# A table set with both Exp and Ln, loaded once per stretch, and 26 more ticks in the Exp form of the gelu

## What is computed

```python
h = rmsnorm(x, norm_mix)
q_sb, k_sb, v_sb, q_sw, k_sw, v_sw, q_mem, gates = split_projection(h, w_in, b_gate)
# stick-breaking attention
log_keep = where(mask, -softplus(z), 0); weight = where(mask, exp(log_sigmoid(z) + log_between), 0)
# windowed attention (softmax with sinks) and attention over memory tokens (softmax)
x = x + merge(o_sb, o_sw, o_mem, gates, w_o_sb, w_o_sw, w_o_mem, w_out)
x = x + peer_ffn(rmsnorm(x, norm_ffn), w_peer_q, peer_keys, peer_u, peer_v)
# peer_block, per row: 8 heads, the 16 best of 128 x 128 experts each
g = softmax(best)
a = gelu(einsum('thkd,td->thk', u_tab[idx], xb))
out = einsum('thk,thkd->td', g * a, v_tab[idx])
```

## Time and profile before

| | us |
|---|---|
| median of 3 runs | 4570.85 |
| lowest, highest | 4563.27, 4574.06 |
| the profiled execution | 4568.99 |
| its span, first to last instruction | 4567.2 |

### The profile page before, as it was taken

How to read it: one execution, slowest core, us unless ns; L and a number is a source line. 1 busy time by engine, 2 the same in 40 slices (tenths; PEclk the granted TensorE clock), 3 DMA queues, 4 the chain that set the end, 5 groups by cost and what they waited for, 6 DMA issues and landing times.

```text
span 4567.2 us, 47872 instructions
## 1 busy us (share of the span) xinstructions
PE 3318.5 (73%) x16665; PEld 1485.3 (33%) x16665; DVE 2543.6 (56%) x6300; ACT 1999.6 (44%) x4853; POOL 1249.0 (27%) x1167
## 2 busy tenths in 40 slices
PE   8988987766666999886775565699988555555555
PEld 4565653222222445432322222244443111111111
DVE  1321148546655674684565645676458577576544
ACT  4531024656887322325567788832232222222222
POOL 0000013212112333332221212233333444444443
PEclk9869998787777999987887777799999776777777
DMA  5222359766655999998865556699999999999999
GB/s 201 68 68 92 128 204 412 286 255 249 217 206 213 401 416 409 413 382 317 307 255 188 215 213 224 248 416 414 415 404 378 412 416 416 416 412 417 417 421 382
DMA packets 230819, 1407.40 MB, mean 308 GB/s; under 512 B 26144, under 2 KB 34080, under 8 KB 77088
## 3 DMA queue, kind: packets, MB, share of 16 engines
q0 software_dynamic: 165888, 1208.03, 66.4%
q1 hardware_dynamic: 64688, 196.30, 11.6%
HBM read 1384.58 MB, written 20.58 MB: 308 GB/s over the span
## 4 chain that ended last, share of the span: by engine, by line
PE 39%; DMA 20%; ACT 18%; DVE 18%; issue 5%; POOL 1%; SPq 0%; DVEq 0%; ACTq 0%; POOLq 0%
DMA ring<-in_experts_dram,idx 20%; PE ps L1177 11%; DVE ring L1740 7%; PE ps L1106 7%; PE ps L911 4%; PE ps L1149 4%; PE ps L1111 4%; PE ps L1126 3%; ACT L1396 3%; ACT L1394 3%; ACT diag L1414 2%; ACT L1316 1%; ACT wgt L1408 1%; PE ps L1084 1%; PE ps L906 1%
## 5 line engine op out<-in xcount | busy, mean ns | idle before, releaser
L1177 PE MATMUL ps<-ring,diag 64*64 64x512 f32 x9216 | 1429.6, 748 | 1001.1 <-ACT diag L1414 984.2
L862 POOL DMA_INDIRECT ring<-in_experts_dram,idx x1152 | 1243.6, 1079 | 3141.5 <-PE ps L1177 2511.7
L1740 DVE CUSTOM_DVE_ANT_0 ring<-ring,xp 128x1024 f32<-128x1024 f32 x1152 | 1389.4, 1224 | 828.0 <-DMA ring<-in_experts_dram,idx 807.8
L1177 PEld LDWEIGHTS ps<-ring,diag 64*64 64x64 f32 x9216 | 351.8, 158 | 1906.4 <-ACT diag L1414 1344.9
L1400 ACT ACTIVATE act_<-hid 128x2 f32<-128x2 f32 x416 | 84.6, 203 | 1632.3 <-DVE hid L1740 1614.5
L1106 PE MATMUL ps<-hx,over 128*128 128x384 f32 x1152 | 400.1, 496 | 7.3 <-DMA over<-in_w_gate_o_dram 7.3
L1414 ACT ACTIVATE diag<-const,wgt 128x64 f32<-128x64 f32 x1152 | 337.9, 340 | 18.8
L911 PE MATMUL ps<-over,hx 128*128 128x512 f32 (+1 forms) x720 | 314.5, 590 | 0.0
L1106 PEld LDWEIGHTS ps<-hx,over 128*128 128x128 f32 x1152 | 214.4, 191 | 202.4 <-issue 70.8
L1149 PE MATMUL ps<-hx,over 128*128 128x384 f32 x768 | 264.6, 494 | 1.2 <-ACT hx L1352 1.2
L1531 DVE SCALAR_TENSOR_TENSOR over<-ps,over 128x512 f32<-128x512 f32 x76 | 52.6, 692 | 300.7 <-ACT over L1316 292.1
(11 more groups left out here) (217 smaller groups left out, 3336.9 us busy)
## 6 DMA issues: line engine op xcount, KB each, us to landing
over<-in_w_gate_o_dram SPq DMA_DIRECT2D x72, 768.0 KB
over<-in_w_in_dram SPq DMA_DIRECT2D x15, 2048.0 KB
over<-in_w_q_dram SPq DMA_DIRECT2D x24, 1024.0 KB
ring<-in_experts_dram,idx POOLq DMA_INDIRECT x1152
over<-in_w_out_dram SPq DMA_DIRECT2D x12, 1024.0 KB
oq<-in_x_prompt_dram SPq DMA_DIRECT2D x16, 512.0 KB, 15.6
x_scratch<-oq SPq DMA_DIRECT2D x9, 512.0 KB
over<-in_w_mem_kv_dram SPq DMA_DIRECT2D x2, 2048.0 KB
```

Source lines behind the costliest of these rows:

```text
L862: i = nc.gpsimd.indirect_dma_start(out=ring[:, j % RING, :], out_offset=None, in_=A["experts"], in_offset=bass.IndirectOffsetOnAxis(ap=idx ...
L1177: last = nc.tensor.matmul(acc[ROWS[r ^ h], h, :], diag[ROWS[r], j % 4, :], ring[ROWS[r], j % RING, DM + h * HB:DM + (h + 1) * HB], start=( ...
L1740: last = nc.vector.tensor_tensor_reduce(out=rows, in0=rows, in1=xp[:, :], scale=1.0, scalar=0.0, op0=ALU.mult, op1=ALU.add, accum_out=hid[ ...
```

## The change

A set of ACT's tables that has both Exp and Ln, `natural_log_exp_and_others`, is asked for by name at the begin of the program, at each tick where a stretch of the Exp form begins, and in `front` before the second norm's Ln. And `exp_form()` takes the first RANK_LEAD + 2 = 28 ticks too (26 of them had the Gelu form), so the stretches become 0 to 93 and 192 to 283.

```diff
+LOGS = "natural_log_exp_and_others"
...
     for T in range(NT * NB):
         to = done + PACES[1 + T]
-        out.append(any(done <= b and to > a for a, b in spans[1:]))
+        out.append(T < RANK_LEAD + 2 or any(done <= b and to > a for a, b in spans[1:]))
         done = to
...
                     if tau == f.mean_at:
+                        nc.scalar.preload_act_table_set(LOGS)
                         act.wait_ge(meaned, g + 1)
...
             advance = walk(project, attend, front)
+            nc.scalar.preload_act_table_set(LOGS)
             advance(0)
...
                     c = recent(tick)
+                    if EXP_FORM[T] and not (T and EXP_FORM[T - 1]):
+                        nc.scalar.preload_act_table_set(LOGS)
                     act.wait_ge(dots, T + 1)
```

## The result

The changed kernel takes 4212.75 us (median) against 4570.51 us, 0.9218 of it, 95% interval 0.92 to 0.9236. Its profiled execution took 4211.32 us (span 4209.2). The forecast was 4240 with a range of 4150 to 4340: right in direction, 27 us too high. One of the changed kernel's four executions took 6292.23 us, at a granted clock of 1.00, for a reason that nothing here shows; the ratio leaves it out, and without it the median is 4211.32.

What follows compares the result with a forecast made beforehand. Packed transfers bound the first ticks and fronts; in projections and attention ACT's table loads made ticks late. Terms -59 - 56 - 67 - 137 - 9 - 5 + 8 = -325 from 4569 gave 4244, said as 4240, range 4150 to 4340.

Steps and rivals of the forecast that it cites:

- The loads are ACT's time, 1.31 us a switch, and go: Whole kernel: each table switch costs ACT 1.31 us; some 30 of 600 loads stay once one set holds both functions.
- Their worth is what lies on the chain: Each stage gains only its loads on the chain, not all 769.7 us, limited by the busiest other engine's floor.
- Attention 2: Attention of group 2 under the ticks, 589.8 us: chain loads 158.1, DVE floor 438, so -152, taken as -137.
- Attention 1: Attention of group 1 under the ticks, 377.4 us: chain loads 74.3, DVE floor 298, so -74, taken as -67.
- a tenth off: Both attention stretches: gain cut by a tenth because DVE and PE would wait for each other; a choice, not a row.
- The projections' floor: Projections of groups 1 and 2: PE's busy time over 0.92 leaves 233 and 232 us, so -59 and -56.
- Before tick 0: Stretch ahead of the first tick: chain loads of 6.5 and 2.6 us go, -9 us.
- Fronts: Fronts 1 and 2, at `mean_at`: two loads leave, -5 us for both, or 0 where packed DMA takes it back.
- The first 26 ticks: Ticks 0 to 25 switched to the Exp form: +8 us, bounds -3 to +29; 0.4 of DVE's 17.4 us counted.
- Whole chain and faster clock: Rival: all chain loads go and PE's clock rises in denser attention, about 4150 us; 15%.
- Another path close under the chain: Rival: in attention the DVE-PE exchange may hold the ticks, half the loads' time stays, 4390 us; 14%.
- The preload does not hold: Rival: loads still precede every Ln and Exp, first 26 ticks go from 6.1 to 9.4 us, +86, 4655 us; 3%.

Runs made afterwards that it cites:

- e5: Changed kernel with first 26 ticks back in the Gelu form, but DVE still doing its four Exp-form instructions there, results unused: 4204.82 us, 0.9205; that stretch 167.0 us.
- e2: Kernel before the change, with the Exp form in the first 28 ticks and no preload: 4590.31 us, 1.0057 of the kernel before.
- e3: Changed kernel with one load of the already loaded table before the gelu's first Exp in each of 186 Exp-form ticks: 4313.72 us, 0.9456 of the kernel before.

## Why the prediction was right, and where it was off

- **The loads are ACT's time, 1.31 us a switch, and go.** Right: 31 left of 600 (some 30 forecast), and ACT's busy time fell by 717.8 us (1999.6 to 1281.8; 569 loads x 1.283 = 730, less the added ACTIVATEs).
- **Their worth is what lies on the chain.** Right, and it is the step that carried the forecast. But the sums took the loads of the printed part of each row: 60.2, 74.3, 61.4 and 158.1 us where the whole chains hold 69.4, 77.2, 68.1 and 167.0. In three of the four stretches the drop was the whole of that within 5% (72.6, 76.2, 65.6), in attention 2 0.81 of it (136.0).
- **Attention.** Attention 2: 137 forecast, 136.0 measured. Attention 1: 67 forecast with a tenth off, 74 without it, 76.2 measured. The tenth was a choice and not a row; it was wrong in the one and hit in the other, where 152 would have stood without it. That the term of attention 2 came out to 1 us is luck in part.
- **The projections' floor was the most mis-sized term.** The terms added to -325, measured was -358.0: 33 us, 23 of them here (13.6 and 9.6), 9 in attention 1, 10 before tick 0, and 9 back in the fronts and last ticks. I took PE's busy time of before as fixed (214.34 us) and allowed a share of 0.92, which gave 233. PE reached only 0.88 of 219.8, but its busy time fell to 194.42 for the same 887 matmuls. With that time the same floor is 211 us in both projections and binds nothing; the stage less the loads of its whole chain is then 292.4 - 69.4 = 223.0 and 288.1 - 68.1 = 220.0, against 219.8 and 222.5 measured. It took both errors: with the whole row read and the old floor the forecast would still have been 233 and 232. The matmuls' groups in projection 1, before and after:

```profile
L911 PE MATMUL ps<-over,hx 128*128 128x512 f32 (+1 forms) x240 | 109.2, 607 | 0.0
...
L912 PE MATMUL ps<-over,hx 128*128 128x512 f32 (+1 forms) x240 | 99.0, 559 | 0.0
```

  559 ns in place of 607 for each, at a granted clock of 0.95 in place of 0.85. The runs form a row in projection 1: clock 0.85, 0.89, 0.91, 0.93, 0.95 with 214, 205, 201, 199, 194 us of PE, for the kernel before, two gelu loads, the norms' loads, one gelu load, and the changed kernel. The denser the stretch, the higher the clock; that was in the forecast only as a rival's surplus.
- **Before tick 0** 18.7 us went where 9 were forecast: I left out the first 100 us and steps cut off the row. The whole chain of that stretch holds 13 loads, 16.8 us. The stretch scatters by 12 us from run to run, so no more can be said.
- **Fronts.** -5 forecast, about nothing measured (+4.2 us for front 1, the 8 ticks after it, front 2 and the last ticks together). The other bound that I had given, packed transfers that take it back, fits; no run tried it.
- **The first 26 ticks.** +8 forecast, +6.9 measured against the kernel before; that is luck in part, as two misses cancel. The preloads with the Gelu form alone bring the stretch to 155.3 to 155.8 us from 158.6, which the forecast had only as a bound (-3), and against that the Exp form costs 10 to 12 us, not 7 to 8: some 0.8 of DVE's 13.7 us, where the forecast had 0.4 of 17.4. That DVE is the reason is shown by e5 in this stretch.
- **The rivals.** Whole chain and faster clock, 4150: about a third of the way from the forecast to it. In the projections and attention 1 the chain's loads went whole and PE's clock rose, in attention 2 a fifth of them stayed. Another path close under the chain, 4390: no; shares of 0.44 to 0.49 for one load and 0.48 to 0.51 for two show no kink. The preload does not hold: no, and its price was wrong too, e2 gives +27 us where the rival said +86. The Trainium skill (ScalarE activation tables: per-element evaluation and per-set limits, Table sets in the compiler and the runtime) has the back end place the loads, for the longest run. That loads are placed unasked is so here: all 600 of before, and 25 of the 31 after. The longest run is not borne out: before, each Ln and Exp of the gelu got a load of its own where one set would have served, and the six loads that were asked for were kept, and no other stands before a Ln or Exp of the gelu, the softplus chain or the norms.

The version with the preloads and the Gelu form in the first ticks is the best one measured that computes the whole result: 0.9196 and 0.9201 of the kernel before, against 0.9213 to 0.9218 for the change, by a margin about as large as the intervals.

## What to carry to other kernels

Price a removed stall by its share in the chain of its own stretch, stage by stage, over all steps of the chain and not only those that a row prints: here that gave 382 us for the 350 that went. Do not hold the busy time of PE fixed while you make a stretch denser. Where the transfers are packed, do not price by the chain: 77 us of loads on it cost 17. The same stall of 1.28 us cost 0.96 of its length in the norms, half in the gelu and the softplus chain, and a fifteenth to a sixth beside packed or nearly packed transfers. When one edit comes in two parts, time each alone: here the preloads give 0.920 and the form change gives back some 0.002 in total, 10 to 12 us in its own stretch.

## What the runs showed of the hardware

- A load of the set that is already loaded takes the same 1283 ns; none of the 186 in e3 was skipped, and they cost 109 us.
- A switch costs 1.31 us from the end of one ACTIVATE to the start of the next (566 of the 600 in the kernel before took no longer than 1.35 us), with no drain visible beside it.
- The accumulation of a tick on four quadrants of 64x64 took 1.95 us, with two of them left out 1.93 us, at a granted clock of 1.00. The Trainium skill (TensorEngine Tiling (Array Packing), Tiling Modes) says that such tiles work in parallel; these rows agree.
- L1745's operation takes 1224 ns for 1024 columns and 688 ns for 512: 1.05 ns a column and, as an estimate from these two sizes, about 150 ns fixed.
